# One expert round in another order: gate and up products in a row, sums in six units, four weight loads ahead of a row store

## The reference, cut to what matters

```python
def moe_ffn(h, w_rg, b_rg, w_re, b_re, w_g, w_u, w_d):
    ...
    def run(args):
        xe, e = args
        return (jax.nn.silu(xe @ w_g[e]) * (xe @ w_u[e])) @ w_d[e]
    yb = lax.map(run, (xb, blk_expert)).reshape(P, D)
    y_assign = yb[dest].astype(jnp.float32) * flat_w[order][:, None]
    return jax.ops.segment_sum(y_assign, tok_sorted, num_segments=N).astype(h.dtype)
```

## Time and profile before

| | |
|---|---|
| median of 3 runs | 978.51 us (978.45 to 978.81) |
| the profiled execution | 977.84 us |
| its span, first to last instruction | 976.0 us |
| PE busy | 944.1 us (97%) |
| DVE busy | 553.3 us (57%) |
| ACT busy | 190.0 us (19%) |
| moved by DMA | 261.09 MB, mean 268 GB/s |

### The profile page before, as it was taken

The page is one execution under the profiler, slowest core; times in us unless marked ns, Lnnn a source line. Parts: engine busy times, 40 slices in busy tenths (PEclk is TensorE's granted clock), DMA queues, the critical chain, the costliest instruction groups (busy, mean ns, idle before and its releaser), DMA issues.

```text
span 976.0 us, 11301 instructions
## 1 busy us (share of the span) xinstructions
PE 944.1 (97%) x4417; PEld 465.9 (48%) x4417; DVE 553.3 (57%) x1085; ACT 190.0 (19%) x420; POOL 61.4 (6%) x70
## 2 busy tenths in 40 slices
PE   5999999999999999989999999999999999999898
PEld 2575667877654445734333333333333333334443
DVE  2205441446876513466777777777777776677334
ACT  4011221002755311121111111111111111112301
POOL 3010024000000000010000000000000000000000
PEclk9999999999999999999999999999999999999999
DMA  9590353250000791299999999999999999999211
GB/s 288 183 300 17 77 154 111 96 184 23 2 1 21 189 417 73 102 357 409 419 421 419 418 420 419 419 420 420 418 420 420 419 417 421 418 421 389 88 42 50
DMA packets 73242, 261.09 MB, mean 268 GB/s; under 512 B 12202, under 2 KB 36150, under 8 KB 48196
## 3 DMA queue, kind: packets, MB, share of 16 engines
q1 hardware_dynamic: 68560, 251.26, 65.9%
q0 software_dynamic: 4080, 8.93, 2.8%
q10 hardware_dynamic: 548, 0.17, 0.1%
HBM read 253.24 MB, written 13.08 MB: 273 GB/s over the span
## 4 chain that ended last, share of the span: by engine, by line
PE 82%; DMA 10%; SPq 3%; DVE 2%; ACT 1%; issue 1%; ACTq 0%; DVEq 0%
PE ps L1015 73%; DMA w<-in_w_exp_up 6%; SPq L348 3%; DMA w<-in_w_exp_down 3%; PE ps L1374 2%; PE ps L1632 2%; PE ps L1033 1%; DMA hn_rows<-hnt 1%; PE ps L1669 1%; PE ps L1115 1%; PE ps L1116 1%; DVE h L2547 0%; DMA gmix<-in_norm_mix 0%; ACT probs L836 0%; PE ps L1377 0%
## 5 line engine op out<-in xcount | busy, mean ns | idle before, releaser
L1015 PE MATMUL ps<-w,xe 128*64 128x512 f32 x1024 | 233.6, 598 | 5.0 <-DMA w<-in_w_exp_up 4.0
L2504 DVE TENSOR_TENSOR h<-h,ps 128x1024 f32<-128x1024 f32 (+1 forms) x150 | 177.4, 1216 | 31.4 <-PE ps L1015 29.3
L1015 PEld LDWEIGHTS ps<-w,xe 128*64 128x64 f32 x1024 | 69.2, 136 | 139.5 <-issue 135.1
L1015 PE MATMUL ps<-w,hT 128*64 128x512 f32 x512 | 116.9, 599 | 0.7 <-DVE hT L2481 0.5
L1015 PE MATMUL ps<-xT,wring 128*128 128x272 f32 x384 | 101.1, 403 | 0.0
L1015 PE MATMUL ps<-yk,ST 128*128 128x512 f32 (+1 forms) x320 | 95.3, 414 | 0.5 <-DVE yk L2495 0.5
L1015 PE MATMUL ps<-wring,xT 128*32 128x128 f32 (+2 forms) x368 | 79.4, 410 | 1.4 <-DVE xT L391 1.4
L1015 PEld LDWEIGHTS ps<-xT,wring 128*128 128x128 f32 x384 | 68.7, 190 | 25.1 <-issue 12.2
L967 ACT ACTIVATE sg<-ps 64x256 f32<-64x256 f32 x64 | 24.1, 377 | 258.4 <-PE ps L1015 258.0
L684 POOL DMA_INDIRECT xg<-hn_rows,sidx x32 | 32.4, 1014 | 652.0 <-PE ps L1632 368.7
L1015 PEld LDWEIGHTS ps<-w,hT 128*64 128x64 f32 x512 | 34.1, 136 | 66.7 <-issue 66.0
(11 more groups left out here) (343 smaller groups left out, 868.1 us busy)
## 6 DMA issues: line engine op xcount, KB each, us to landing
w<-in_w_exp_gate SPq DMA_DIRECT2D x64, 1024.0 KB, 23.2
w<-in_w_exp_up SPq DMA_DIRECT2D x64, 1024.0 KB, 25.8
w<-in_w_exp_down SPq DMA_DIRECT2D x64, 1024.0 KB, 25.2
wring<-in_w_in SPq DMA_DIRECT2D x12, 512.0 KB, 6.3
wpg<-in_w_ple_gate SPq DMA_DIRECT2D x2, 2048.0 KB, 13.7
biaslines<-blrow SPq DMA_DIRECT2D x1, 2560.0 KB, 11.0
h<-in_x_prompt SPq DMA_DIRECT2D x4, 512.0 KB, 11.6
wring<-in_w_in SPq DMA_DIRECT2D x2, 1024.0 KB, 10.2
```

Source lines behind the costliest of these rows:

```text
L1015: return nc.tensor.matmul(out, l, r, start=start, stop=stop, skip_group_check=skip)
L2504: TTn(h[0:r, t, :], h[0:r, t, :], both(4 + 2 * (t % 2), r), ALU.add).then_inc(S["hadd"], 1)
```

## The change

1. **SP's list before the experts.** The store of tile 3's normed rows (`rows_out(TP - 1)`) moves behind the four weight loads that wait for `op_done`, the last product of the output projection. Before, the store was issued first.
2. **PE's round.** All four parts of `gate_up(J)` come in a row. Then `combine(J-2, 0)`, `rows_T(J+1)`, `combine(J-2, 1)`, `combine(J-2, 2)`, `down(J-1)`, `combine(J-2, 3)`, `combine(J-2, 4)`, `hidden_T(J)`, `combine(J-2, 5)`. The transposes of the hidden rows of expert J are thus in round J, no longer in round J+1.
3. **Six units.** The sample tile is summed in two units of 512 columns each, in bank 1; the prompt tiles keep two banks each. Gate and up sums use bank 0 alone, and `gate_up(J)` waits for `times_up(J-1)`.
4. **DVE's round** is `add 0`, `times_up`, `x_columns`, `add 1`, `add 2`, `spots(J-1)`, `add 3`, `add 4`, `h_columns(J)`, `low_rows(J-1)`, `add 5`.
5. **The end.** `spots(31)` and `low_rows(31)` stand behind the last three adds of expert 29; two of those units stand on PE behind `down(31)`. `final_T(0)` waits for three tiles of `h`, and no longer for four, and uses banks 2 and 3.

```diff
+        UNITS = ((0, None), (1, None), (TP, 0), (2, None), (3, None), (TP, 1))
+        NU = len(UNITS)
+
+        UNIT_OF = (1, 2, 4, 5, 6)
+
+        def unit_banks(u):
+            t, half = UNITS[u]
+            return (4 + 2 * (t % 2), 2) if half is None else (1, 1)
...
-            for t in range(TP):
+            for t in range(TP - 1):
                 rows_out(t)
             sp.wait_ge(S["op_done"], TT)
             load_piece(sp, 1, D0, 1)
             for i in (U0, G1, U1):
                 load_piece(sp, 2, i, 2)
+            rows_out(TP - 1)
             rows_out(TP)
             load_piece(sp, 1, D1, 1)
...
                 act.wait_ge(S["d_done"], J + 1)
                 if not isinstance(J, int):
-                    act.wait_ge(S["comb"], J * TT)
+                    act.wait_ge(S["comb"], J * NU)
                 elif J >= 2:
-                    act.wait_ge(S["comb"], (J - 1) * TT)
+                    act.wait_ge(S["comb"], (J - 1) * NU)
...
-                    if not isinstance(J, int):
+                    if not isinstance(J, int) or J:
                         pe.wait_ge(S["hm_ok"], J)
-                    elif J >= 2:
-                        pe.wait_ge(S["hm_ok"], J - 1)
                 if part % 2 == 0:
                     pe.wait_ge(S[f"wl{slot}{'ab'[half]}"], landings(J))
                 for c in range(2 * part, 2 * part + 2):
                     j = c % 4
                     for k, i in enumerate(((G0, U0), (G1, U1))[half]):
-                        last = mm(ps[k * SLOTS:(k + 1) * SLOTS, b, :], xe[:, b, j, half * SLOTS:(half + 1) * SLOTS],
+                        last = mm(ps[k * SLOTS:(k + 1) * SLOTS, 0, :], xe[:, b, j, half * SLOTS:(half + 1) * SLOTS],
...
-            def combine(J, t):
-
-                r = rows(t)
-                if t == 0:
+            def combine(J, u):
+
+                t, half_ = UNITS[u]
+                r, (b, n_) = rows(t), unit_banks(u)
+                if u == 0:
                     pe.wait_ge(S["st_ok"], J * 2 + 2)
                     pe.wait_ge(S["lo_ok"], J + 1)
 
-                if t != 1 and (not isinstance(J, int) or J or t):
-                    pe.wait_ge(S["hadd"], J * TT + max(t - 1, 0))
-                if t == 0 and not isinstance(J, int):
+                if not isinstance(J, int) or J or u >= 3:
+                    pe.wait_ge(S["hadd"], J * NU + (u - 2))
+                if u == 0 and not isinstance(J, int):
                     pe.sem_inc(S["passed"], 1)
-                for half in range(2):
-                    last = mm(ps[0:r, 4 + 2 * (t % 2) + half, :], ST[:, two(J), t * P:t * P + r],
-                              yk[two(J)][:, half * 512:(half + 1) * 512], True, True)
+                for k in range(n_):
+                    c0 = (k if half_ is None else half_) * 512
+                    last = mm(ps[0:r, b + k, :], ST[:, two(J), t * P:t * P + r], yk[two(J)][:, c0:c0 + 512], True, True)
...
             rows_T(0)
-            for J in range(NE):
-                gate_up(J, 0)
-                gate_up(J, 1)
-                if J:
-                    hidden_T(J - 1)
+            def regular(J):
+                for part in range(4):
+                    gate_up(J, part)
                 if J >= 2:
                     combine(J - 2, 0)
-                    combine(J - 2, 1)
-                gate_up(J, 2)
-                gate_up(J, 3)
                 if J + 1 < NE:
                     rows_T(J + 1)
                 if J == 0:
                     slot_lines()
+                if J == 2:
+                    pe.wait_ge(S["jei_ok"], 1)
+                if J >= 2:
+                    combine(J - 2, 1)
+                    combine(J - 2, 2)
+                if J:
+                    down(J - 1, 0)
+                    down(J - 1, 1)
+
+            for J in range(NE - 1):
+                regular(J)
                 if J == 1:
                     slot_sums(1, hotV, RV, 7, 2 * MAXOV)
                 if J >= 2:
-                    combine(J - 2, 2)
                     combine(J - 2, 3)
-                if J:
-                    down(J - 1, 0)
-                    down(J - 1, 1)
+                    combine(J - 2, 4)
+                hidden_T(J)
                 if J >= 2:
-                    combine(J - 2, 4)
+                    combine(J - 2, 5)
...
             L = NE - 1
+            regular(L)
             hidden_T(L)
+            combine(L - 2, 3)
             down(L, 0)
             down(L, 1)
+            combine(L - 2, 4)
+            combine(L - 2, 5)
             pe.wait_ge(S["lo_ok"], L)
             pe.wait_ge(S["st_ok"], 2 * L)
-            pe.wait_ge(S["hadd"], (L - 1) * TT + TP)
+            pe.wait_ge(S["hadd"], (L - 1) * NU - 1)
             combine_two(L - 1, 0)
-            pe.wait_ge(S["hadd"], L * TT)
+            pe.wait_ge(S["hadd"], L * NU)
             combine_two(L - 1, 1)
...
-                pe.wait_ge(S["hadd"], n * TT + (max(t, 3 * (t == 0)) + 1 - TT))
+                pe.wait_ge(S["hadd"], n * NU + (UNIT_OF[2] - NU if t == 0 else 0))
                 pe.sem_inc(S["passed"], 1)
                 if t >= 2:
                     pe.wait_ge(S["f_hpT"], t - 1)
-                token_T(t, h[0:rows(t), t, :], 2 * (t % 2), S["f_tr"])
+                token_T(t, h[0:rows(t), t, :], 2 - 2 * (t % 2), S["f_tr"])
...
-            def add(J, t):
-
-                r = rows(t)
-                dve.wait_ge(S["comb"], J * TT + (t + 1))
-                TTn(h[0:r, t, :], h[0:r, t, :], both(4 + 2 * (t % 2), r), ALU.add).then_inc(S["hadd"], 1)
+            def add(J, u, n=1):
+                t, half = UNITS[u]
+                r, (b, n_) = rows(t), unit_banks(u)
+                dve.wait_ge(S["comb"], J * NU + (u + 1))
+                if half is None:
+                    TTn(h[0:r, t, :], h[0:r, t, :], both(b, r), ALU.add).then_inc(S["hadd"], 1)
+                else:
+                    part = h[0:r, t, half * 512:(half + 1) * 512]
+                    TTn(part, part, ps[0:r, b, :], ALU.add).then_inc(S["hadd"], n)
...
             for J in range(NE):
                 if J >= 2:
-                    low_rows(J - 2)
-                if J:
-                    h_columns(J - 1)
-                if J >= 2:
                     add(J - 2, 0)
-                    add(J - 2, 1)
-                if J:
-                    spots(J - 1)
+                times_up(J)
                 if J + 1 < NE:
                     x_columns(J + 1)
-                times_up(J)
                 if J == 0:
                     dve.wait_ge(S["db_ps"], 1)
...
+                if J >= 2:
+                    add(J - 2, 1)
+                    add(J - 2, 2)
+                if J == NE - 1:
+                    break
+                if J:
+                    spots(J - 1)
+                if J >= 2:
+                    add(J - 2, 3)
+                    add(J - 2, 4)
+                h_columns(J)
+                if J:
+                    low_rows(J - 1)
+                if J >= 2:
+                    add(J - 2, 5)
...
             L = NE - 1
             h_columns(L)
+            spots(L - 1)
             low_rows(L - 1)
-            add(L - 2, TP)
-
-            dve.sem_inc(S["hadd"], TT)
+            add(L - 2, 3)
+            add(L - 2, 4)
+
+            add(L - 2, 5, 1 + NU)
```

More of the change, by code:

```diff
@@ L966, in gated @@
                 for k in range(2):
-                    last = A(sg[k * SLOTS:(k + 1) * SLOTS, b, :], ps[0:SLOTS, b, k * 256:(k + 1) * 256], ACT.Silu)
+                    last = A(sg[k * SLOTS:(k + 1) * SLOTS, b, :], ps[0:SLOTS, 0, k * 256:(k + 1) * 256], ACT.Silu)
                 last.then_inc(S["silu_ok"], 1)
@@ L1678, in down @@
                     elif J:
-                        pe.wait_ge(S["hm_ok"], J)
+                        pe.wait_ge(S["hm_ok"], J + 1)
                     else:
@@ L1773, in job @@
                     down(J, part)
-                for t in range(TT):
-                    combine(J, t)
+                for u in range(NU):
+                    combine(J, u)
             n = overflow(pe, nov, job)
             def final_T(t):
-                pe.wait_ge(S["hadd"], n * TT + (max(t, 3 * (t == 0)) + 1 - TT))
+                pe.wait_ge(S["hadd"], n * NU + (UNIT_OF[2] - NU if t == 0 else 0))
                 pe.sem_inc(S["passed"], 1)
@@ L2530, in _ @@
                     indices(NE, MAXOV, 1, 7, "jei_ok")
-                if J >= 2:
-                    for t in range(2, TT if J < NE - 1 else TP):
-                        add(J - 2, t)
                 if J == 2:
@@ L2545, in _ @@
                 r, b = rows(t), last_banks(t)
-                dve.wait_ge(S["comb"], L * TT - TT + 2 * (t + 1))
-                TTn(h[0:r, t, :], h[0:r, t, :], both(b, r), ALU.add).then_inc(S["hadd"], 1)
+                dve.wait_ge(S["comb"], (L - 1) * NU + 2 * (t + 1))
+                TTn(h[0:r, t, :], h[0:r, t, :], both(b, r), ALU.add).then_inc(S["hadd"], 1 + (t == 2))
             def job(J):
@@ L2554, in job @@
```

(6 more changed lines are left out.)

12 lines of the change are left out of this document (6 added, 6 removed).

## The result

| | before | after |
|---|---|---|
| median of the runs, us | 978.66 (978.45 to 980.37) | 990.76 (989.42 to 991.1) |
| profiled execution, time / span, us | 977.84 / 976.0 | 990.55 / 988.7 |
| expert 0's first product, us | 435.40 | 446.74 |
| first `down(31)` product, us | 893.15 | 903.07 |
| first `wpg` product of the end, us | 906.90 | 919.63 |

The recorded ratio of the two kernels is 1.0116, 95% interval 1.0100 to 1.0132; the two medians divided by each other give 1.0124, 12.1 us. So the kernel after is 1.2% slower, some 11 to 12 us. The prediction was 989.3 us (984.5 to 991.5).

A forecast was written before the change was run, and what follows sets the result against it. The prediction took the expert stage to be bound by its weight stream, started by expert 3's first load. 977.84 + 6.4 (hold after absorption) + 1.5 (clock) + 2.9 (tail) = 988.6, plus 0.67 for the median: 989.3 us, range 984.5 to 991.5.

The forecast's parts named there:

- What bounds the stage: Expert stage: it ends when its last byte arrives, about 892 us, counted from the issue of expert 3's first load at 439.09.
- Each round may grow by 1.3 us before anything is lost: Expert rounds: PE takes 14.3 us and DMA 15.6 us, so growth up to 1.3 us a round costs nothing.
- Nor does a shorter round gain: Expert rounds: shortening PE's round brings no time; the new order was costed at nothing.
- The hold, 7.2 us: Before the experts: DVE stands 7.2 us longer (5.2 to 7.5) before tile 4's `hnt`, until tile 3's store lands.
- What PE's wait absorbs, 0.8 us: Before `slot_sums`: PE's existing 0.82 us wait absorbs 0.8 of the hold, leaving expert 0 6.4 us late.
- The clock, 1.5 us: PE's pause before the experts: the throttled clock behind it adds 1.5 us (0 to at most 1.7).
- Bytes loaded earlier than that bring nothing: Weight loads before expert 3's: issuing them earlier gains nothing, since the fourth expert's load has to wait for PE.
- The tail, 2.9 us: Behind `down(31)`: DVE's longer list starts the last sums 5.2 us behind the product; costs 2.9 us (0 to 3.3).
- the clock did fall: Answers a rival on the front pause: the clock stays full, giving 987.8 us; chance 20%.
- the tail wasn't hidden: Answers a rival on the end: DVE catches up or the half-speed window moves, giving 986.4 us; chance 14%.
- the store was held up: Answers a rival on tile 3's store: it passes the loads, landing by about 412, giving 980.6 us; chance 10%.
- no round of the kernel after reached 15.6 us: Answers a rival on the rounds: a DVE wait lengthens each beyond 15.6 us, giving 992 us and more; chance 6%.

The follow-up runs named there:

- second run of the changed kernel with its own buffer: Changed kernel with a separate buffer for tile 4's normed rows, measured once more on one chip with two other versions: 978.27 us, ratio 0.9996.
- the version with the other end: Changed kernel with tile 4's own rows buffer, expert 29's sums ahead of `down(31)` and DVE's last steps reordered: 978.91 us, ratio 0.9969; again 976.70 us, 0.9979.
- third group: One of three groups of runs made on three chips; the kernel before had a median of 979.04 us in it.
- second group: One of three groups of runs made on three chips; the kernel before had a median of 982.58 us in it.

## Why the prediction was right, step by step

- **What bounds the stage.** Right in kind: the stream ends it, expert 3's first load starts it (450.44 - 439.09 = 11.35 us later in the profiled pair, the same as expert 0's 11.34), and the chain ends in a landing. Wrong in the cover. "Each round may grow by 1.3 us before anything is lost" took the difference of two rates for slack. What counts is the difference of two ends, 457.75 and 452.65: PE spends its head start on the way, and 5 us are left over all rounds. It did no harm here only because the new round is shorter. "Nor does a shorter round gain" held: 9.9 us of PE's list brought nothing.
- **The hold, 7.2 us.** Mechanism right, and shown from both sides, by the kernel with the late store alone and by the own buffer. The size was 8.14. The first load went when forecast (405.76 - 1.35 = 404.41, against 404.45), but the 4.72 MB took 420.04 - 405.76 = 14.3 us to the landing instead of 13.3: I had divided bytes by the mean rate of a stretch that looked alike, and it ran at 330 GB/s instead of 354.
- **What PE's wait absorbs, 0.8 us.** Right: `slot_sums` begins without a wait.
- **The clock, 1.5 us.** Mechanism right, shown by the products in the pause; the term that was mis-sized: 2.67 by the trace. I had taken the loss of eight products from the earlier trace rows only; the rank products between `asn` and them ran at half clock as well, and the clock was still at 0.50 in 434:435, 5 us after PE had begun again. The start of the program was also a poor witness: its products are slow there at a granted clock of 1.00, so only the 0.50 of the earlier trace rows bore on the term.
- **The early loads.** "Bytes loaded earlier than that bring nothing" stays half open. The own buffer with early loads brings 2.9 to 3.1 us, and of these 1.5 to 2 are DVE's wait for the store, which I hadn't looked at as something to gain. For the new round the claim is borne out: its stretch from expert 0 to `down(31)` is 456.87 us with the store first and 456.99 with early loads and the same buffer of its own. For the old round there is only the one 457.75, and no run here tells whether the rest is the early loads.
- **The tail, 2.9 us.** 2.81 in the trace, 5.22 us behind the product as forecast; the 3.1 us of the kernel with the store first and the 2.1 us between the two kernels with their own buffer lie on either side of it. The stretch of half clock fell on `wpg` again (8.83 us for sixteen products, as in the earlier trace rows), so nothing came back there. The prediction was right to allow for it, though: with the same tail and the clock at 1.00 throughout it, these products took 7.13 us in the second run of the changed kernel with its own buffer, 1.7 us less, and 10.03 in that of the version with the other end.
- **The sum.** The errors were +0.94 (hold), +1.17 (clock), -1.42 (stream), -0.1 (tail): together +0.6 on a forecast of 10.8 us. The 1.35 us of the program's start belong to the one execution and to no term. That the median came out within 1.5 us owes something to errors of both signs.

The rivals: the clock did fall; the tail wasn't hidden; the store was held up (landing at 420.0, not by 412); no round of the kernel after reached 15.6 us.

Of the two rules weighed in the prediction, that of the Trainium skill, "DMA: Bandwidth & Descriptors", section "Queues, rings and completion order", held here in its first half only: the 11.06 us of the store show a queue taken in order, and no trace here shows a small store that finishes ahead of the loads in front of it. "TensorE: Matmul & The Clock Gate", section "What's actually happening", agrees with the windows: 0.50 in the pause and behind it, 1.00 there when the ten products fill it.

## What to carry to other kernels

Before a store is moved behind loads in one queue, look for who waits for its landing to use the buffer again: behind four loads of 1 MB it landed 11 us after its issue here instead of 3, and a second small buffer made the same early loads a gain (0.3%) instead of a loss (0.9%). Where a stream and an engine's list end within a few us of each other, the cover of either is the difference of their ends over the whole stage, not the difference of their rates times the rounds; a kernel with the bytes cut and one with the work padded give both ends. And an engine's pause is priced with its clock: here 8 us of wait cost 2.7 us more, which ten idle products took away.

## What was unexpected in the hardware

- The clock can fall in a pause as short as one that left it alone in another execution. In the kernel with the store first again PE waited 1.93 us for `cum`, about as long as the 1.95 of the earlier trace rows, but its windows show

```profile
420.00:421.00 1.00, 0.00 (x0) 0.00 (x0) 0.86 (x5) 0.00 (x0) 0.00 (x0) 1.00 1.04 442
421.00:423.00 2.00, 1.61 (x8) 1.55 (x8) 0.78 (x4) 0.12 (x1) 0.00 (x0) 0.69 0.99 414
423.00:425.00 2.00, 2.00 (x4) 1.03 (x4) 0.86 (x5) 1.98 (x4) 0.00 (x0) 0.50 1.04 438
```

  and expert 0 began 37.1 us behind the quarters instead of 34.7. In the kernel before the clock was 1.00 throughout there. The same place can cost 2.4 us or nothing.
- This is seen in the times as well. Of the 29 executions of the kernel before in the third group, the nine with a mean granted clock of 0.993 took 979.65 to 980.57 us, the two with 0.997 took 975.90 and 976.34. Differences of 1 to 3 us between kernels are worth comparing at equal clock.
- The program's first eight products took 5.1 to 6.6 us in the traces of kernels that are alike up to there, and the whole program shifts with it: outside the second group the quarters begin between 400.67 and 402.24 us, in the order of these durations. On the second group's chip they begin at 404.13 to 405.46. Two profiled executions may thus differ by 1.6 us on like chips, and by up to 4.8 us on unlike ones, before the change has acted; landmarks are best counted from one that lies just ahead of the change.
- A DMA share near 1 doesn't show that the loads bind. With one sixth of the bytes gone it is still 0.99, at 381 GB/s and with PE waiting for no load; the prediction had read much from 1.01.
- A store of 0.52 MB took 11.06 us from issue to landing behind 4.2 MB of loads in its queue (the chain of the kernel after has it), and about 3 us with none ahead (407.53 to 410.55).
